# Sixteen instead of fourteen of 22 weight pairs by seven products, in two up stages of a transformer kernel

## The reference, cut to what matters

```python
D_FF = -(-8 * D_MODEL // (3 * 256)) * 256          # 2816

def swiglu_ffn(h, w_in, w_out):
    gate, up = jnp.split(jnp.einsum('bsd,df->bsf', h, w_in), 2, axis=-1)
    return jnp.einsum('bsf,fd->bsd', jax.nn.silu(gate) * up, w_out)
...
        hn = rmsnorm(h, norm_gains[layer, 2])
        h = h + rmsnorm(swiglu_ffn(hn, ffn_w_in[layer], ffn_w_out[layer]), norm_gains[layer, 3])
```

## Time and profile before

| what | value |
|---|---|
| median of 3 runs | 2321.96 us (2321.89 to 2322.27) |
| profiled execution, first to last instruction | 2320.9 us, 1.1 under the median |
| TensorE busy | 2309.1 us, 99% |
| VectorE busy | 1498.3 us, 65% |
| ScalarE busy | 1119.0 us, 48% |
| GpSimd busy | 223.6 us, 10% |
| granted TensorE clock | 1.000 of full speed |
| first up stage: first unit to first down product | about 255 to 472.6 us |

### The profile page before, as it was taken

One profiled execution on the slowest core, in us unless ns is written; L12 is line 12 of the kernel. 1 busy time (PEld: TensorE's weight loads), 2 busy tenths in 40 slices (PEclk: granted clock), 3 DMA queues, 4 the chain that ended last, 5 costly groups with the idle time before them and its releaser, 6 DMA issues.

```text
span 2320.9 us, 32131 instructions
## 1 busy us (share of the span) xinstructions
PE 2309.1 (99%) x12088; PEld 1950.9 (84%) x12088; DVE 1498.3 (65%) x2173; ACT 1119.0 (48%) x1829; POOL 223.6 (10%) x313
## 2 busy tenths in 40 slices
PE   9999999999999999999999999999999999999999
PEld 8777889988888888999888778888888878888887
DVE  6665789952738968899428876777434456777731
ACT  6655544452539965445326854444323444544420
POOL 1221013200125410232000000000001000000000
PEclk9999999999999999999999999999999999999999
DMA  5433223332242222333322223323322323233232
GB/s 167 152 132 102 85 92 109 104 112 93 87 118 64 64 84 82 99 110 111 113 89 77 64 82 91 100 90 106 100 93 91 100 69 95 91 100 100 95 107 79
DMA packets 72541, 226.30 MB, mean 98 GB/s; under 512 B 7921, under 2 KB 19489, under 8 KB 72417
## 3 DMA queue, kind: packets, MB, share of 16 engines
q1 hardware_dynamic: 67840, 210.72, 28.5%
q0 software_dynamic: 4576, 13.89, 1.9%
HBM read 221.28 MB, written 2.18 MB: 96 GB/s over the span
## 4 chain that ended last, share of the span: by engine, by line
PE 92%; DVE 3%; ACT 3%; POOL 1%; issue 1%; DMA 0%; DVEq 0%; ACTq 0%; SPq 0%
PE bank L338 26%; PE bank L340 25%; PE bank L339 25%; PE bank L478 5%; PE bank L470 4%; PE bank L1605 1%; PE bank L1596 1%; PE bank L1639 1%; DVE w_lo L312 0%; DVE h L756 0%; POOL hgrn_lv L2560 0%; PE bank L2651 0%; PE bank L2015 0%; POOL hgrn_lv L2547 0%; PE bank L3103 0%
## 5 line engine op out<-in xcount | busy, mean ns | idle before, releaser
L312 DVE TENSOR_TENSOR w_lo<-raw,w_hi 128x1024 fp32r<-128x1024 f32 (+1 forms) x310 | 402.3, 1308 | 218.4 <-ACT w_hi L307 218.1
L338 PE MATMUL bank<-x_hi,w_hi 128*128 128x512 f32 x1344 | 529.2, 394 | 1.2 <-ACT sb_q L2761 1.0
L340 PE MATMUL bank<-x_hi,w_lo 128*128 128x512 f32 x1344 | 523.4, 389 | 0.0
L339 PE MATMUL bank<-x_lo,w_hi 128*128 128x512 f32 x1344 | 523.1, 389 | 0.0
L307 ACT ACTIVATE w_hi<-raw 128x1024 fp32r<-128x1024 f32 (+1 forms) x310 | 344.6, 1121 | 179.9 <-PE bank L340 93.5
L338 PEld LDWEIGHTS bank<-x_hi,w_hi 128*128 128x128 f32 x1344 | 252.3, 188 | 57.4 <-issue 3.1
L340 PEld LDWEIGHTS bank<-x_hi,w_lo 128*128 128x128 f32 x1344 | 252.2, 188 | 53.0
L339 PEld LDWEIGHTS bank<-x_lo,w_hi 128*128 128x128 f32 x1344 | 252.5, 188 | 51.2 <-issue 0.5
L338 PE MATMUL bank<-st_a_hi,w_hi 128*128 128x512 f32 (+1 forms) x396 | 145.1, 366 | 0.0
L340 PE MATMUL bank<-st_a_hi,w_lo 128*128 128x512 f32 (+1 forms) x396 | 144.7, 365 | 0.0
L1374 DVE TENSOR_TENSOR bank<-bank,rstd 128x512 f32<-128x512 f32 x120 | 83.2, 696 | 92.2 <-PE bank L340 92.2
(11 more groups left out here) (444 smaller groups left out, 4673.2 us busy)
## 6 DMA issues: line engine op xcount, KB each, us to landing
raw<-in_w_up SPq DMA_DIRECT2D x120, 512.0 KB, 3.5
raw<-in_w_down SPq DMA_DIRECT2D x64, 704.0 KB, 4.2
st_raw_even<-in_w_up SPq DMA_DIRECT2D x28, 512.0 KB, 4.2
st_raw_odd<-in_w_up SPq DMA_DIRECT2D x24, 512.0 KB, 4.0
raw<-in_w_fox_qk SPq DMA_DIRECT2D x16, 512.0 KB, 3.7
raw<-in_w_hgrn_qf SPq DMA_DIRECT2D x16, 512.0 KB, 3.5
fox_c_keys_a<-fox_c_rows POOLq DMA_DIRECT2D x8, 640.0 KB, 4.1
fox_c_keys_b<-fox_c_rows POOLq DMA_DIRECT2D x8, 640.0 KB, 4.5
```

The costliest lines, as they stand in the source:

```text
L312: nc.vector.tensor_tensor(w_lo[:, slot, 0:size], raw[:, slot % 2, 0:size], w_hi[:, slot, 0:size].bitcast(F32), ALU.subtract).then_inc(sem( ...
L338: nc.tensor.matmul(out, w[0], x[0], start=first, stop=False)
L339: nc.tensor.matmul(out, w[0], x[1], start=False, stop=False)
L340: return nc.tensor.matmul(out, w[1], x[0], start=False, stop=last)
```

## The change

ST_PAIRS goes from 14 to 16 and ST_FIRST from 8 to 6 in each of the two stages. The preparation that lay beside plain tiles 3 to 7 lies beside tiles 3 to 5, `st_mix` gets a place of its own behind `st_xn`, ORDER_X has form 2 ahead of form 4, and TensorE no longer waits once for all seven forms but for each form before the part that uses it. The last plain tile now uses the PSUM banks of the first seven-product pair, so part 0 waits for the gate of tile 4 and part 3 for the gate of tile 5. GpSimd's first sum no longer waits for the forms.

```diff
@@ -128,7 +128,7 @@
 
     with ExitStack() as ctx:
         sems = {}
-        ST_ALL = 2 * (FT - 8)
+        ST_ALL = 2 * (FT - 6)
 
         SHARED = {
             "gla_kdt": ("fx_turned", 2 * FOX_PAIRS), "gla_o": ("fx_pv", FOX_PAIRS), "gla_ds": ("fx_scores", 8 * FOX_PAIRS),
@@ -249,7 +249,8 @@
         st_out = nc.alloc_sbuf_tensor_at("st_out", [P, 4, PAIR_T], F32, offset=at_sq + 8 * T)
         st_two = nc.alloc_sbuf_tensor_at("st_two", [P, 2, PAIR_T], F32, offset=at_sq + 16 * T)
         st_sum = nc.alloc_sbuf_tensor_at("st_sum", [P, 2, T], F32, offset=at_sq)
-        st_mix = nc.alloc_sbuf_tensor_at("st_mix", [P, QUAD, PAIR_T], F32, offset=at_sq)
+        st_mix = nc.alloc_sbuf_tensor_at("st_mix", [P, QUAD, PAIR_T], F32, offset=arena + 4 * T * (ST_FIRST + DT))
+        assert ST_FIRST + DT + 2 <= A_MAIN
 
         def st_raw_pair(n):
 
@@ -921,18 +922,20 @@
             acc = st_acc(n)
 
             def part(i, out):
+                if not n:
+                    pe.wait_ge(sem("st_xlo"), 7 * f + ORDER_X.index(i) + 1)
                 for k in range(QUAD):
                     w = [st_w(n, h, slice(i, i + 1))[:, 0, k * P:(k + 1) * P] for h in range(2)]
                     ins = mm3(out, w, [form_hi[i][:, k, :], form_lo[i][:, k, :]], not k, k == QUAD - 1)
                 return ins
-            if not n:
-                pe.wait_ge(sem("st_xlo"), 7 * f + 7)
-            pe.wait_ge(sem("gated_ready"), FT * f + (ST_FIRST + n - 2 if n > 1 else 5 + 2 * n) + 1 + 2)
+            pe.wait_ge(sem("gated_ready"), FT * f + ST_FIRST + n - 2 + 1 + 2)
             pe.wait_ge(sem("st_lo"), 5 * g + 1)
             part(0, acc[0]).then_inc(sem("st_part"), 1)
             part(1, acc[1])
             pe.wait_ge(sem("st_lo"), 5 * g + 2)
             part(2, acc[2]).then_inc(sem("st_part"), 1)
+            if not n:
+                pe.wait_ge(sem("gated_ready"), FT * f + ST_FIRST - 1 + 1 + 2)
             part(3, acc[3])
             pe.wait_ge(sem("st_lo"), 5 * g + 3)
             part(4, acc[4]).then_inc(sem("st_part"), 1)
@@ -961,7 +964,7 @@
                         pe_unit_k(c, up_bank(j, c), range(2, DT))
                     else:
                         pe_unit(pe, s, c, u + c, up_bank(j, c))
-            for j in (1, 2, 3):
+            for j in range(1, ST_FIRST // 2 if f < 2 else 4):
                 up_body(j, u_of(f"up{f}") + 4 * j, False)
             if f < 2:
                 for n in range(ST_PAIRS):
@@ -1155,7 +1158,7 @@
                     n = FT * f + ft
                     if f < 2:
                         up_ahead(convert_act, act, f, j, 2 * p, u, last)
-                        if ft == 7:
+                        if ft == ST_FIRST - 1:
                             act_forms(act, f, (6,))
                             act.wait_ge(sem("unit_used"), u + 2 + CREDIT)
                             act_pair(act, f, 0, "a")
@@ -1164,13 +1167,11 @@
                         act.wait_ge(sem("scaled"), 2 * (n - unscaled(f)) + 1)
                         nc.scalar.activation(silu[:, p, :], ps[up_bank(j, 2 * p)][:], ACT.Silu).then_inc(sem("silu_ready"), 1)
                         up_ahead(convert_act, act, f, j, 2 * p + 1, u, last)
-                        if ft == 4:
-                            act_forms(act, f, (0, 3))
-                        if ft == 5:
-                            act_forms(act, f, (1, 4))
-                        if ft == 6:
-                            act_forms(act, f, (2, 5))
-                        if ft == 7:
+                        if ft == ST_FIRST - 3:
+                            act_forms(act, f, (0, 3, 1))
+                        if ft == ST_FIRST - 2:
+                            act_forms(act, f, (2, 4, 5))
+                        if ft == ST_FIRST - 1:
                             used(act, u + 2)
                             act_pair(act, f, 0, "s3")
                             act_pair(act, f, 0, "g")
@@ -1222,7 +1223,7 @@
             b21, b22 = (st_xn[:, QUAD:DT, half] for half in HALVES)
             dve.wait_ge(sem("st_form"), 5 * f + {3: 1, 4: 2, 2: 2, 6: 4}[i])
             if i in (2, 6):
-                dve.wait_ge(sem("st_xlo"), 7 * f + {2: 2, 6: 5}[i])
+                dve.wait_ge(sem("st_xlo"), 7 * f + {2: 2, 6: 4}[i])
             if i == 3:
                 ins = nc.vector.tensor_tensor(st_mix[:], b11, b12, ALU.subtract)
             elif i == 4:
@@ -1236,7 +1237,7 @@
             dve.wait_ge(sem("st_xhi"), 7 * f + ORDER_X.index(i) + 1)
             nc.vector.tensor_tensor(form_lo[i][:], form_of(i), form_hi[i][:].bitcast(F32), ALU.subtract).then_inc(sem("st_xlo"), 1)
 
-        ORDER_X = (0, 3, 1, 4, 2, 5, 6)
+        ORDER_X = (0, 3, 1, 2, 4, 5, 6)
 
         def pool_ffn(pool, s):
             f = s // 2
@@ -1246,8 +1247,6 @@
                 st_raw_wait(pool, f, n, 1)
                 if n:
                     pool.wait_ge(sem("st_lo"), 5 * (g - 1) + 2)
-                else:
-                    pool.wait_ge(sem("st_xlo"), 7 * f + 7)
                 nc.gpsimd.tensor_tensor(st_sum[:, 1, :], rg[:, 0, :], rg[:, 1, :], ALU.add).then_inc(sem("st_pool"), 1)
                 st_raw_wait(pool, f, n, 0)
                 if n:
@@ -1390,11 +1389,6 @@
                         conv_ahead(convert_dve, dve, f, j, p, 0)
                     else:
                         up_ahead(convert_dve, dve, f, j, 2 * p, u, last)
-                        if ft == 7:
-                            dve_sums(dve, f, 0, True)
-                            dve_pair(dve, f, 0, "s3")
-                            dve_pair(dve, f, 0, "g")
-                            dve_pair(dve, f, 0, "s4")
                     if f >= 2 and not (isinstance(ft, int) and ft == 0):
                         low_part(ft - 1, 1 - p)
                     if f >= 2:
@@ -1406,19 +1400,17 @@
                         up_ahead(convert_dve, dve, f, j, 2 * p + 1, u, last)
                         if ft == 3:
                             dve_normed(dve, f, s)
-                        if ft == 4:
-                            dve_forms(dve, f, 3)
-                            dve_forms(dve, f, 4)
+                        if ft == ST_FIRST - 2:
                             dve_form_lo(dve, f, 0)
                             dve_form_lo(dve, f, 3)
-                        if ft == 5:
                             dve_forms(dve, f, 2)
                             dve_form_lo(dve, f, 1)
-                            dve_form_lo(dve, f, 4)
-                        if ft == 6:
-                            dve_form_lo(dve, f, 2)
-                            dve_forms(dve, f, 6)
+                        if ft == ST_FIRST - 1:
                             dve_form_lo(dve, f, 5)
+                            dve_pair(dve, f, 0, "a")
+                            dve_sums(dve, f, 0, False)
+                            dve_form_lo(dve, f, 6)
+                            dve_pair(dve, f, 0, "s12")
                         scale(1)
                     dve.wait_ge(sem("silu_ready"), n + 1)
                     if f < 2:
@@ -1429,11 +1421,18 @@
                         second = conv_g[:]
                     out = gated[:, p, :] if f >= 2 else a_plain(ft)
                     nc.vector.tensor_tensor(out, silu[:, p, :], second, ALU.mult).then_inc(sem("gated_ready"), 1)
-                    if f < 2 and ft == 6:
-                        dve_form_lo(dve, f, 6)
-                        dve_pair(dve, f, 0, "a")
-                        dve_sums(dve, f, 0, False)
-                        dve_pair(dve, f, 0, "s12")
+                    if f < 2 and ft == ST_FIRST - 3:
+                        dve_forms(dve, f, 3)
+                        dve_forms(dve, f, 4)
+                    if f < 2 and ft == ST_FIRST - 2:
+                        dve_form_lo(dve, f, 2)
+                        dve_form_lo(dve, f, 4)
+                        dve_forms(dve, f, 6)
+                    if f < 2 and ft == ST_FIRST - 1:
+                        dve_sums(dve, f, 0, True)
+                        dve_pair(dve, f, 0, "s3")
+                        dve_pair(dve, f, 0, "g")
+                        dve_pair(dve, f, 0, "s4")
             if f < 2:
                 for j in range(ST_FIRST // 2):
                     up_body(j, u_of(f"up{f}") + 4 * j, False)
```

## The result

| | before | after |
|---|---|---|
| median, lowest to highest of 13 runs each | 2322.34 us, 2321.84 to 2324.47 | 2327.18 us, 2326.21 to 2328.54 |
| profiled execution / its span | see above | 2326.83 / 2324.9 us |

The ratio is 1.002, with a 95% interval of 1.0013 to 1.0028. The changed kernel is 4.8 us slower, 0.21%, just past the bound of what can be told from no change. The forecast was 2324.1 us with a range to 2326.2. The direction was forecast; the time came out 3.1 us above it and 1.0 above the range.

The account below looks back on a forecast made before the run. TensorE's own instruction stream was taken to bound the kernel, with little slack on VectorE. Two stalls of 2.7 us less the 3.2 us gain made +2.1 us, so 2324.1 us, with an 8-in-10 range of 2321.5 to 2326.2.

Parts of the forecast that it names:

- Gain 3.2 us: On TensorE, four pairs go from plain form to seven products, saving 0.80 us each, as an upper bound.
- First wait 2.7 us a stage: TensorE stalls at each stage's first seven-product matmul: 1.7 us from VectorE's queue, 2.7 with GpSimd's sum holding form 2's split.
- That margin holds: At pair 1's first weights: VectorE ends at 320.5, 2.0 us before TensorE's need, so no wait was counted.
- The walk of VectorE's queue: VectorE's instructions timed in their new order from tile 3's gate, to place when each weight block is ready.
- rival B: GpSimd's pair 1 sum also holds pair 0's last block, part 5 waiting 0.7 us more; 2325.5 us, chance 0.20.
- The small margins inside pair 0: Parts 2 and 3 of pair 0 have 0.1 to 0.2 us to spare; counted as nothing, up to 0.3 as bound.
- Rival D: TensorE's clock falls to its lower level after the stall, 4 us at it in each stage; 2328.1 us, chance 0.07.
- the prediction's own signs of being wrong: TensorE waiting in later pairs, GpSimd's sums running while VectorE is idle, or the clock leaving 1.00 behind the stall.
- The chance of 0.89 for no measurable change: Whole kernel: probability given to a time within 0.2% of before, with 0.09 for slower and 0.02 for faster.

Follow-up runs that it names:

- experiment 5: Against experiment 4's kernel: VectorE itself makes the sums of pairs 0 and 1 that GpSimd made; 2320.06 us.
- experiment 6: Against the changed kernel: low parts of forms 2, 4, 5 and 6 left out, high parts multiplied in their place; 2320.71 us.
- experiment 1: Against the changed kernel: GpSimd's two sums for pair 0 wait until the low part of pair 0's first weights is made; 2329.92 us.
- experiment 2: Against the changed kernel: TensorE does 22 unused matmuls just before it waits for pair 0's first weights; 2327.03 us.
- experiment 7: Against the changed kernel: TensorE waits once for all seven forms before part 0, as the kernel before did; 2331.58 us.
- experiment 8: Against the changed kernel, order kept: VectorE instead of GpSimd makes the sums of pairs 0 and 1; 2325.07 us.
- experiment 3: Against the changed kernel: VectorE makes form 0's low part earlier, in its gap before unit 10; 2326.93 us.
- experiment 4: Against the changed kernel: work ordered by TensorE's need, pair 1's weights loaded earlier, GpSimd's pair 1 sums held until pair 0's weights finish; 2324.85 us.

## Why the prediction came out as it did

- **Gain 3.2 us: right in kind, perhaps a little small.** The losses of both stages less the measured difference from before give the gain back: 3.9 in experiment 5, 3.8 in experiment 6, 3.5 for the change, and 3.1 to 4.5 over all ten kernels. Single profiles differ by 1.1 elsewhere, and what lies between 3.2 and the middle of these, 3.9, is open.
- **First wait 2.7 us a stage: right** at 2.87 and 2.79, with 1.7 of queue (1.67 without the collision, experiment 1) and the rest GpSimd. The instruction that was held was the low part of form 4, not of form 2: GpSimd's second sum came later than walked, first waited for form 2 and then blocked form 4, and the price is about the same, 1.1. That the right price came from the wrong instruction is part luck. The last link of the chain is ScalarE's: VectorE idles 0.34 before the first weights, whose high part stands behind form 6's in ScalarE's queue. The rule of the Trainium skill (page SBUF — State Buffer, section Who interferes with whom), that the loser of such a meeting fully blocks, fits every held row: 2.31 is 1.22 and 1.09 of standing still, and in experiment 5, where GpSimd is silent, 1.22 is back.
- **The step that failed is "That margin holds": the sum has no term for what comes behind the first wait.** The walk of VectorE's queue ended at the first weight block of pair 1, put at 320.5 with 2.0 us to spare. The block began at 319.89, against 320.5 − 1.22 = 319.3 in the walk, and 0.49 of that is a shift that was there before the stage's new part began (TensorE was ready at 310.24, not 309.75). But it took 2.30 instead of 1.22 and ended at 322.19, 1.0 before TensorE wanted it. So that block was in time. The ones behind it, which the walk didn't reach, were not: GpSimd's two sums of pair 1 hold VectorE for 2.2 us, and "s12" ended at 326.25, wanted at 326.07. I had looked for one such meeting (rival B) at the last block of pair 0 and priced it at 0.7. Behind its first wait each stage lost another 4.42 − 2.87 = 1.55 us (nearly all of it slow clock) and 3.94 − 2.79 = 1.15 us (nearly all of it waits in pair 1). These 2.7 us, taken at nothing in the sum, are as large as the gap between 2.1 forecast and 4.8 measured. The two first waits were also 0.3 longer in all than forecast, so the terms add up to 5.2; the 0.4 too much is the same open point as at the gain. The small margins inside pair 0 did hold: in the second stage they cost 0.06 us.
- **Rival D: half seen, wrongly priced.** The clock did fall, in one stage of two in this execution, and cost 1.5 there. I made it an addition on top of all waits. In the change it isn't, as experiment 2 shows: without it waits take its place. In experiment 7, where no wait was left behind the first one, it is. "Nothing in the rows shows the clock ever falling" was true of before, where no idle time in these stages comes near 2.7 us, and so said nothing on what one would do. Two of the prediction's own signs of being wrong came: TensorE waits in a later pair, and the clock leaves 1.00.
- **The chance of 0.89 for no measurable change was too high.** +2.1 forecast and 4.6 as bound left 2.5 us, 1.25 a stage, and the loss that I had left out was of that size.
- **Not settled:** whether the clock falls at an idle time of this length. It fell after 2.71, 2.52, 2.49 and 2.42 us (the last in both stages of experiment 1), not after 2.63, nor after the 1.52 at the first wait in experiments 1 and 8. The length of the idle time was not varied by itself.

## What to carry to other kernels

When a change makes an already full engine late, the wait at the first consumer is not the bill. Walk the late engine's queue until it has idle time again, and count at each step what another engine takes from it; in experiments 2 and 3 the losses changed their place and form while the time stayed within 0.3 us, and in experiment 4 the first waits went away, 5.7 us for both stages, but only 2.4 us of loss with them. An instruction given to a second engine to relieve the first is relief only if they don't meet: where they met, 0.6 to 0.8 us of addition handed to GpSimd cost VectorE 1.1. And in these runs a slow clock was hidden only where the engine would have waited anyway. And two remedies that each look half good can be worth far more together, so try the square.

## What the runs showed of the hardware

GpSimd and VectorE, both with instructions in line, take turns: two sums of GpSimd (1.29 each alone) held two instructions of VectorE for 1.0 to 1.1 us each at pair 1 in the first stage of the change, and at pairs 0 and 1 in experiments 3 and 4. VectorE's scaling out of PSUM at 303.63 was not held beside GpSimd's sum at 303.96.

TensorE's granted clock went to 0.50 some 1.4 us after work began again behind an idle time of 2.71, for 16 distances of 0.21 us between matmuls instead of 0.12, while TensorE was busy; one execution did it in one stage and not in the other. In experiment 7, with idle times of 4.34 and 4.43 us, it was at 0.50 before work began again, and stayed for 13 slow distances in one stage and 27 in the other.
